# Expert rows combined at the end: the last two tiles by products on TensorE, the other row loads after the third-last tile

## The chip, the core and the metric

The kernel runs on one NeuronCore of a Trainium2 chip. Its engines are PE (TensorE, matrix products), DVE (VectorE), ACT (ScalarE), POOL (GpSimd) and SP (SyncE, which here only issues DMAs); 16 DMA engines move data between HBM and SBUF. The metric is the time of the whole program on the device in microseconds (us), as a median of several executions. "Span" is the time from the first to the last instruction of the one execution that was profiled.

## What is computed

A one-layer encoder block on 512 tokens of width 1024 in float32: RMS norm, a projection, a convolution branch and a sparse attention branch, gates, an output product, and then a mixture of experts, with a last RMS norm. What matters here is the end:

```
h = rms_norm(x, g_ffn)
x = x + hier_moe(h, ...)        # each token: 1 of 4 groups, 2 of its 8 experts
return rms_norm(x, g_final)

# hier_moe, for each token t and its two experts e with weights c[t, e]:
#   y[t] += c[t, e] * (silu(h[t] @ w_gate[e]) * (h[t] @ w_up[e])) @ w_down[e]
```

Each of the 32 experts has w_gate and w_up of 1024 x 256 and w_down of 256 x 1024.

## The kernel before, in words

Tokens stand in four blocks of 128 (TB = 4, one token per partition); `xr` ("x_rows") is the residual in SBUF, `wts[:, c, b]` the weight of choice c (0 or 1) of the tokens of block b. DVE computes the routing: for each token and choice the slot in a *tile*. A tile has 32 slots for each expert of a pair, so one tile serves one pair of experts; a pair has at least one tile, and there are 16 pairs. In this run 30 tiles are used. `tab[n]` is the number of tiles up to pair n in the order of work, read into registers by the engines ("TENSOR_LOAD tab"); `order` is the order of the pairs. The weights of a pair (4 MB for gate and up in eight loads of 512 KB, 2 MB for down in two of 1 MB) go into one of three slots; SP issues the loads of pair n when PE has finished with the pair n-3 (L400 and L410).

For each tile t, in a loop on every engine:
- POOL gathers the tokens' rows by an indirect DMA into `ring` ("bm", L582), some tiles ahead. Its tiny additions on `carrier` (L567) carry signals.
- DVE copies them to `xg` ("v_rows", L1608 for the first tile, L1613 in the loop). PE transposes them (L909), ACT and DVE evacuate half each (L1218, L1602, "kT").
- PE multiplies by gate and up (L932), ACT takes SiLU (L1225), DVE multiplies and so on (L1616, L1619), PE transposes once more (L941) and multiplies by down (L949) into `bank[2]`, of which each quarter of 32 partitions holds one expert's 32 slots by one half of 512 columns.
- ACT evacuates `bank[2]` to `ys` ("qT", L1229). POOL scatters it by an indirect DMA to `y_dram` ("expert_rows", L622), which has a row for each choice and token (row c * 512 + token). Indices beyond the bound write nothing; that is how empty slots are left out.

After the last tile (`tiles` in all):
- SP loads the final gain (L451, earlier, once the last pair but one has its tiles done), waits until the scatters of *all* tiles have landed (L454), loads the eight blocks of expert rows into `yrow` ("region", L457), and stores each block of the result when it is ready (L463).
- DVE adds `wts * yrow` to `xr` for each block and choice (L1627, 128 x 1024), and scales the finished block by `rs` and the gain (L1637): the left half, and the whole for the last block.
- ACT squares and sums a block (L1232) and scales right halves of blocks 0 to 2 (L1237), POOL computes the power -0.5 (L628) and multiplies those right halves by the gain (L633).
- PE has nothing to do.

The engines run their own programs in order and wait on semaphores. The order is that of the code; there is no scheduler.

## Time and profile before

| | |
|---|---|
| median of 3 executions | 682.74 us (681.72 to 686.35) |
| the profiled execution | 684.94 us, span 683.0 us |
| PE busy | 561.7 us, 82% of the span |
| DVE, ACT, POOL busy | 337.5, 256.9, 299.3 us |
| DMA moved | 149.21 MB |
| expert tiles, by PE's first and last instruction of them | 405.9 to 649.0 us |

Busy time is the time in which an engine executes instructions. A row of a timeline gives the start of an instruction (or of several alike), its duration, the engine, the line of the kernel and what it writes and reads. In brackets stands the idle time of the engine before it and what released it. SPq is SP's issuing of DMAs; its duration says nothing on when the data lands.

### The profile page before, as it was taken

The numbers are of one execution on the slowest core, as the hardware profiler recorded it, in microseconds if no ns is written. First come the engines' busy times: TensorE is split into PE (matmuls) and PEld (weight loads), VectorE is DVE, ScalarE is ACT, GpSimd is POOL, SyncE is SP. The second block draws the span as 40 slices with busy tenths as digits, with TensorE's granted clock in tenths as the row PEclk, the third lists the DMA queues.
The fourth block names the chain that finished last, engine by engine and source line by source line (L and its number), as shares of the span: only waits on it lengthen the run. The fifth ranks groups of instructions, "written<-read, shape, count | busy, mean of one in ns | idle before, by whom it ended". The sixth has DMA issues, their size and how long they took to land.

```text
span 683.0 us, 12246 instructions
## 1 busy us (share of the span) xinstructions
PE 561.7 (82%) x4275; PEld 380.6 (56%) x4276; DVE 337.5 (49%) x827; ACT 256.9 (38%) x440; POOL 299.3 (44%) x470
## 2 busy tenths in 40 slices
PE   3899999999999999999998218889889859697700
PEld 3577788876665777777888114444444424344300
DVE  4418999999988993477131641121211111021136
ACT  6335433245565746533224002334324314132212
POOL 5334334479995213355700043444534514333314
PEclk9999999999999998999996559999999989899955
DMA  9122723232202033034068978999899999999463
GB/s 293 40 92 63 240 68 108 78 89 74 74 13 62 1 123 124 9 116 154 4 243 322 412 279 319 408 407 410 310 409 410 408 408 409 401 408 390 189 249 124
DMA packets 58813, 149.21 MB, mean 218 GB/s; under 512 B 8660, under 2 KB 25044, under 8 KB 58782
## 3 DMA queue, kind: packets, MB, share of 16 engines
q1 hardware_dynamic: 53438, 139.89, 54.8%
q0 software_dynamic: 5200, 8.41, 3.4%
q10 hardware_dynamic: 144, 0.52, 0.3%
q8 instruction: 16, 0.26, 0.2%
q14 instruction: 15, 0.12, 0.0%
HBM read 145.37 MB, written 12.08 MB: 231 GB/s over the span
## 4 chain that ended last, share of the span: by engine, by line
PE 51%; DVE 19%; SPq 14%; DMA 6%; issue 5%; ACT 3%; POOL 2%; DVEq 0%; ACTq 0%; POOLq 0%
PE bank L667 26%; SPq L400 10%; PE bank L932 9%; PE bank L949 5%; DVE bm L1317 4%; DVE m L1316 4%; SPq L410 3%; DMA region<-in_w_e_down 3%; DVE conv_buf L1308 3%; PE bank L745 2%; PE bank L909 2%; PE bank L880 2%; PE bank L778 1%; PE bank L766 1%; DMA region<-expert_rows 1%
## 5 line engine op out<-in xcount | busy, mean ns | idle before, releaser
L667 PE MATMUL bank<-h_hi,w_part 128*128 128x512 f32 (+1 forms) x528 | 174.8, 400 | 3.2 <-DVE h_lo L1266 1.7
L517 POOL TENSOR_TENSOR w_part<-region,w_part 128x1024 fp32r<-128x1024 f32 (+1 forms) x52 | 109.7, 2111 | 149.2 <-ACT w_part L983 149.2
L667 PEld LDWEIGHTS bank<-h_hi,w_part 128*128 128x128 f32 (+1 forms) x528 | 98.3, 186 | 31.1 <-issue 8.2
L932 PE MATMUL bank<-region,kT 128*32 128x256 f32 x1536 | 94.0, 399 | 18.1 <-DMA region<-in_w_e_up 13.6
L667 PE MATMUL bank<-h_lo,w_part 128*128 128x512 f32 (+1 forms) x264 | 103.6, 392 | 0.0
L1616 DVE TENSOR_TENSOR mask_b<-mask_b,bank 128x128 f32<-128x128 f32 x30 | 8.6, 288 | 187.0 <-ACT mask_b L1225 99.4
L932 PEld LDWEIGHTS bank<-region,kT 128*32 128x32 f32 x1536 | 56.2, 115 | 63.1 <-issue 40.9
L983 ACT ACTIVATE w_part<-region 128x1024 fp32r<-128x1024 f32 (+1 forms) x52 | 48.0, 925 | 109.6 <-PE bank L667 109.4
L567 POOL TENSOR_TENSOR carrier<-mhalf 128x1 f32<-128x1 f32 x184 | 33.0, 196 | 122.8 <-ACT qT L1229 115.8
L1351 DVE SCALAR_TENSOR_TENSOR bank<-glu,cv,bank 128x256 f32<-128x256 f32 x196 | 78.6, 479 | 0.0
L949 PE MATMUL bank<-region,mask_b 128*32 128x512 f32 x384 | 46.2, 598 | 11.7 <-DVE mask_b L1619 10.8
L667 PEld LDWEIGHTS bank<-h_lo,w_part 128*128 128x128 f32 (+1 forms) x264 | 49.3, 187 | 9.9 <-issue 0.7
L1229 ACT ACTIVATE qT<-bank 128x512 f32 x30 | 17.9, 597 | 85.7 <-PE bank L949 85.7
L582 POOL DMA_INDIRECT bm<-h_rows,gi x35 | 37.2, 1064 | 5.3 <-issue 0.5
L1225 ACT ACT_TABLE_LOAD x30 | 38.5, 1283 | 0.5
L1225 ACT ACTIVATE mask_b<-bank 128x128 f32<-128x128 f32 x30 | 8.3, 277 | 77.9 <-PE bank L932 77.9
L622 POOL DMA_INDIRECT expert_rows<-qT,si x30 | 31.0, 1033 | 14.6 <-issue 14.6
L909 PE MATMUL bank<-ident,v_rows 128*128 128x128 f32 x124 | 23.5, 313 | 7.6 <-DVE v_rows L1608 7.6
L909 PEld LDWEIGHTS bank<-ident,v_rows 128*128 128x128 f32 x124 | 17.4, 209 | 20.1 <-issue 20.1
L949 PEld LDWEIGHTS bank<-region,mask_b 128*32 128x32 f32 x384 | 10.4, 109 | 30.2 <-issue 29.2
L525 POOL TENSOR_SCALAR bm<-glu,cv 128x512 f32<-128x512 f32 x17 | 26.6, 1565 | 0.9
L667 PE MATMUL bank<-o_part,w_part 128*128 128x512 f32 x96 | 25.9, 430 | 0.7 <-POOL w_part L517 0.7
(253 smaller groups left out, 864.2 us busy)
## 6 DMA issues: line engine op xcount, KB each, us to landing
region<-in_w_e_down SPq DMA_DIRECT2D x22, 1024.0 KB
region<-in_w_e_gate SPq DMA_DIRECT2D x44, 512.0 KB
region<-in_w_e_up SPq DMA_DIRECT2D x44, 512.0 KB
region<-in_w_in SPq DMA_DIRECT2D x16, 1024.0 KB, 6.0
gates<-in_w_e_gate SPq DMA_DIRECT2D x20, 512.0 KB
gates<-in_w_e_up SPq DMA_DIRECT2D x20, 512.0 KB
conv_buf<-in_w_e_down SPq DMA_DIRECT2D x10, 1024.0 KB
region<-in_w_out SPq DMA_DIRECT2D x2, 2048.0 KB, 7.8
```

The source lines that it names most:

```text
L400: sp.dma_start(w_gu[slot][:, e, m, half, :, :], w[0, bass.ds(pair * 2 + e, 1), rows, :].rearrange("a (p k) f -> p (a k) f", k=KD // 2))\
L517: g.tensor_tensor(unit_part(u, 1), unit_raw(u), unit_part(u, 0).bitcast(F32), ALU.subtract)\
L567: ins = g.tensor_tensor(carrier[:, n:n + 1], mhalf[:], mhalf[:], ALU.add)
L582: g.indirect_dma_start(out=ring[:, u, :], out_offset=None, in_=h2_halves, in_offset=bass.IndirectOffsetOnAxis(ap=gi1[:, u:u + 1], axis=0), ...
L622: g.indirect_dma_start(out=y_halves, out_offset=bass.IndirectOffsetOnAxis(ap=si1[:, q:q + 1], axis=0), in_=ys[:, q, :], in_offset=None, bo ...
L667: last = mm(out_, a_parts[p], b_parts[q], start=start and x_ == 0, stop=stop and x_ == 2)
L909: last = tr(bank[6 + k // 2][:, k % 2 * P:(k % 2 + 1) * P], view[:, k, :], ident[:])
L932: last = mm(bank[0][32 * c:32 * c + 32, 0:FF], xTs[:, k, at_:at_ + 32], w_gu[slot][:, e, :, half, k, j * P:(j + 1) * P], start=(half == 0 ...
L949: last = mm(bank[2][32 * c:32 * c + 32, :], hidT[:, at_:at_ + 32], w_dn[slot][:, e, j, n * BANK:(n + 1) * BANK], start=(j == 0), stop=(j = ...
L983: a(unit_part(u, 0), unit_raw(u), ACT.Copy).then_inc(S["w_hi"], 1)
L1225: a(sil, bank[0][:, 0:P], ACT.Silu).then_inc(S["silu_g"], 1)
L1351: ins = v.scalar_tensor_tensor(out_, shifted, cv[:, c, j:j + 1], so_far, ALU.mult, ALU.add)
```

## The change

What it does, part by part:
- **Routing, DVE.** `tab` gets one more entry, `early` = tiles - 2. Ahead of the first tile DVE takes the scatter indices of the last two tiles to `late_si` and makes their entries in `sidx` invalid, so that these two tiles' scatters write nothing. It clears a tile `no_rows` and builds `col_w`: for each block of tokens a 128 x 128 matrix with a token's weight at the column of its slot in the last two tiles.
- **POOL** writes zeros by two indirect DMAs to the rows of `y_dram` that belong to the last two tiles (semaphore `zeroed`), ahead of its loop. After the tiles it keeps the power alone.
- **PE** transposes `col_w` ahead of the first tile (ACT evacuates it to `place`). After the last tile it forms, for the blocks 0 to 2, `diag` (weights of choice 1 on a diagonal) times the rows of choice 1, and adds `place` times the rows of the last two tiles (`late`); for block 3 the latter alone. Each block is two products of 512 columns into two banks.
- **ACT** builds three `diag` ahead of the first product, evacuates the last two tiles to `late` in four pieces of 32 partitions, and keeps the squares at the end.
- **SP** waits for the scatters of all tiles but the last two, and for `zeroed`, and loads the rows; each load has a semaphore of its own. The last block is stored in two halves.
- **DVE** at the end adds the rows of choice 0 of all blocks and of choice 1 of block 3, adds the banks in halves of 512 columns, and does all of the scaling.

```diff
@@ sync
-            tiles = sp.value_load(tab[0:1, PAIRS:PAIRS + 1], min_val=PAIRS, max_val=MAXT - 1)
+            early = sp.value_load(tab[0:1, PAIRS + 1:PAIRS + 2], min_val=PAIRS - 2, max_val=MAXT - 3)
...
-                sp.wait_ge(scattered[n], ((tiles + (RING - 1 - n)) // RING) * 16)
+                sp.wait_ge(scattered[n], ((early + (RING - 1 - n)) // RING) * 16)
+            sp.wait_ge(zeroed, 32)
...
-            for b in range(TB):
+            for b in range(TB - 1):
                 sp.wait_ge(S["o_ready"], b + 1)
-                if b < TB - 1:
-                    sp.wait_ge(S["o_half"], b + 1)
                 sp.dma_start(out[0, b * P:(b + 1) * P, :], xr[:, b, :]).then_inc(st_out, 16)
+            for n in range(RING):
+                sp.wait_ge(scattered[n], ((early + 2 + (RING - 1 - n)) // RING) * 16)
+            for n in range(2):
+                sp.wait_ge(S["o_ready"], TB + n)
+                sp.dma_start(out[0, (TB - 1) * P:T, n * BANK:(n + 1) * BANK],
+                             xr[:, TB - 1, n * BANK:(n + 1) * BANK]).then_inc(st_out, 16)
@@ gpsimd
             gather(RING, 0)
+            pool.wait_ge(S["late_ready"], 1)
+            hold(5)
+            for u in range(2):
+                g.indirect_dma_start(out=y_halves,
+                                     out_offset=bass.IndirectOffsetOnAxis(ap=late_si[:, u:u + 1], axis=0),
+                                     in_=no_rows, in_offset=None,
+                                     bounds_check=last_row, oob_is_err=False).then_inc(zeroed, 16)
...
-                if b:
-                    pool.wait_ge(ld_gbc, 32)
-                    pool.wait_ge(S["o_scaled"], b)
-                    g.tensor_tensor(xr[:, b - 1, BANK:D], xr[:, b - 1, BANK:D], g_final_bc[:, BANK:D], ALU.mult)\
-                        .then_inc(S["o_half"], 1)
@@ tensor
+            pe.wait_ge(S["col_ready"], 1)
+            for b in range(TB):
+                last = tr(bank[5][:, b * P:(b + 1) * P], col_w[:, b, :], ident[:])
+            last.then_inc(S["place_mm"], 1)
             pe.wait_ge(S["x2_ev"], 2 * TB)
             transpose_tile(0)
...
+            def weighted_row(b):
+                pe.wait_ge(ld_y[b][1], 16)
+                if b == 2:
+                    pe.wait_ge(S["xtev_a"], early + 3)
+                    pe.wait_ge(S["xtev_v"], early + 3)
+                for n in range(2):
+                    mm(bank[late_banks[2 * b + n]][:], diag[:, b, :], y_row(b, 1)[:, n * BANK:(n + 1) * BANK],
+                       start=True, stop=False)
+            def late_rows(b):
+                for n in range(2):
+                    if late_banks[2 * b + n] == 2:
+                        pe.wait_ge(S["yev_a"], early + 3)
+                    mm(bank[late_banks[2 * b + n]][:], place[:, b * P:(b + 1) * P], late[:, n, :],
+                       start=(b == TB - 1), stop=True).then_inc(S["late_mm"], 1)
+            weighted_row(0)
+            weighted_row(1)
+            pe.wait_ge(S["yev_a"], early + 3)
+            late_rows(0)
+            late_rows(1)
+            weighted_row(2)
+            late_rows(2)
+            late_rows(3)
@@ scalar
+            act.wait_ge(S["place_mm"], 1)
+            a(place, bank[5][:], ACT.Copy).then_inc(S["place_ev"], 1)
             rows_T(0)
+            for b in range(TB - 1):
+                last = a(diag[:, b, :], ident[:], ACT.Copy, scale=wts[:, 1, b:b + 1])
...
+            for u in range(2):
+                hidden_gate(early + u)
+                for n in range(2):
+                    for e in range(2):
+                        at_ = 64 * u + 32 * e
+                        last = a(late[at_:at_ + 32, n, :], bank[2][32 * (2 * e + n):32 * (2 * e + n) + 32, :], ACT.Copy)
+                last.then_inc(S["yev_a"], 1)
@@ vector
+            v.tensor_copy(late_si[:], sidx[:, bass.ds(early, 2)])
...
+            v.memset(no_rows, 0.0).then_inc(S["late_ready"], 1)
+            link(v.tensor_tensor(col_hit, spread(col_code, 1, 2 * TB), spread(hic[:], 2, P), ALU.is_equal))
+            link(v.tensor_tensor(col_hit, col_hit, spread(wts[:, :, :].rearrange("p c b -> p (c b)"), 2, P), ALU.mult))
+            v.tensor_tensor(col_w, col_hit[:, 0:TB, :], col_hit[:, TB:2 * TB, :], ALU.add)\
+                .then_inc(S["col_ready"], 1)
...
+            for b in range(3):
+                add_row(b, 0)
+            for k in range(2):
+                add_late(k)
+            add_row(3, 0)
+            for k in range(2, 4):
+                add_late(k)
+            add_row(3, 1)
+            mean_square(2, 0)
+            dve.wait_ge(ld_gbc, 32)
+            scale_out(0, whole)
+            for k in range(4, 6):
+                add_late(k)
+            mean_square(2, 1)
+            scale_out(1, whole)
...
```

Three places of the built programs, engine by engine in program order. The first is DVE ahead of the first tile. Before the change, behind the weights (`wts`) stand a table load and the copy of the first gathered rows (bm to v_rows):

```order
L1597 TENSOR_TENSOR wts<-wts,glu 128x4
L1606 TENSOR_LOAD tab
L1606 ISA x2
L1608 COPY v_rows<-bm 128x512
L1602 COPY kT<-bank 128x256
```

In the changed kernel, behind its own table load and the copy to `late_si`, the same copy (now L1693) is preceded by these; qT holds `col_code`, `col_hit` and `col_w`, glu `no_rows`:

```order
L1673 TENSOR_SCALAR qT<-iota 128x32 x4
L1675 TENSOR_SCALAR hic<-hi,tend 128x8
L1676 SCALAR_TENSOR_TENSOR hic<-hic,posc 128x8
L1677 TENSOR_SCALAR dst<-iota,tend 128x48
L1678 SCALAR_TENSOR_TENSOR sidx<-dst,sidx 128x48
L1679 MEMSET glu 128x512
L1680 TENSOR_TENSOR qT<-qT,hic 128x1024
L1681 TENSOR_TENSOR qT<-qT,wts 128x1024
L1682 TENSOR_TENSOR qT<-qT 128x512
L1693 COPY v_rows<-bm 128x512
```

The copy of the first rows has moved behind nine further kinds of instructions. The second place is PE behind the last tile. It ended there before; in the changed kernel (region is `yrow` or `late`, glu is `diag` or `place`):

```order
L975 MATMUL bank<-region,mask_b 32x512 x8
L947 REGISTER_ALU
L947 COMPARE_AND_BRANCH
L986 TENSOR_LOAD tab
L986 ISA x2
L997 MATMUL bank<-region,glu 128x512 x4
L1010 REGISTER_ALU
L1005 MATMUL bank<-region,glu 128x512 x4
L997 MATMUL bank<-region,glu 128x512 x2
L1005 MATMUL bank<-region,glu 128x512 x4
```

Fourteen products of 128x512 are added. The third place is DVE at the end. Before the change (region is `yrow` or the gain, ss the mean of squares):

```order
L1627 SCALAR_TENSOR_TENSOR x_rows<-region,wts,x_rows 128x1024 x3
L1255 TENSOR_SCALAR ss<-ss 128x1
L1627 SCALAR_TENSOR_TENSOR x_rows<-region,wts,x_rows 128x1024
L1637 SCALAR_TENSOR_TENSOR x_rows<-x_rows,rs,region 128x512
L1627 SCALAR_TENSOR_TENSOR x_rows<-region,wts,x_rows 128x1024
L1255 TENSOR_SCALAR ss<-ss 128x1
```

and in the changed kernel:

```order
L1714 SCALAR_TENSOR_TENSOR x_rows<-region,wts,x_rows 128x1024 x3
L1722 TENSOR_TENSOR x_rows<-x_rows,bank 128x512 x2
L1714 SCALAR_TENSOR_TENSOR x_rows<-region,wts,x_rows 128x1024
L1722 TENSOR_TENSOR x_rows<-x_rows,bank 128x512 x2
L1714 SCALAR_TENSOR_TENSOR x_rows<-region,wts,x_rows 128x1024
L1324 TENSOR_SCALAR ss<-ss 128x1
L1728 SCALAR_TENSOR_TENSOR x_rows<-x_rows,rs,region 128x1024
L1722 TENSOR_TENSOR x_rows<-x_rows,bank 128x512 x2
L1324 TENSOR_SCALAR ss<-ss 128x1
L1728 SCALAR_TENSOR_TENSOR x_rows<-x_rows,rs,region 128x1024
```

Five whole-row adds stand where eight were, all of them ahead of the first scaling; the adds from the banks have come between, and the scaling takes whole rows.

## Rows read from the trace of the kernel before

**Rows 1.** The page: mean busy share of the DMA engines, tenths, 40 slices of 17.1 us.

```profile
DMA  9122723232202033034068978999899999999463
```

**Rows 2.** The chain that ended last, 560 to 684 us: start, us, what.

```profile
578.80 0.27 SPq L440
...
628.27 18.65 DMA region<-in_w_e_down
```

**Rows 3.** Stretches of one microsecond: busy time (count) by engine, PEclk, DMA share, GB/s.

```profile
640.00:641.00 1.00, 0.00 (x0) 0.00 (x0) 0.00 (x0) 0.98 (x2) 0.19 (x1) 1.00 0.45 176
...
646.00:647.00 1.00, 0.20 (x1) 0.00 (x1) 0.52 (x2) 0.02 (x1) 0.00 (x0) 1.00 0.06 25
...
665.00:666.00 1.00, 0.00 (x0) 0.00 (x0) 0.82 (x2) 1.00 (x3) 0.05 (x1) 0.50 0.62 250
666.00:667.00 1.00, 0.00 (x0) 0.00 (x0) 1.00 (x1) 0.41 (x1) 0.00 (x0) 0.50 0.03 12
```

**Rows 4.** Timeline of the end, all engines: start, us, engine, line, operation [idle before].

```profile
634.13 1.03 POOL L622 DMA_INDIRECT expert_rows<-qT,si  x1 [0.49 <-issue]
...
647.05 1.92 PE L949 MATMUL bank<-region,mask_b 128*32 128x512 f32 x16 [0.86 <-DMA region<-in_w_e_down]
...
649.17 0.60 ACT L1229 ACTIVATE qT<-bank 128x512 f32 x1 [3.15 <-PE bank L949]
...
653.52 3.87 SPq L457 DMA_DIRECT2D region<-expert_rows  x8
...
658.42 2.60 DVE L1627 SCALAR_TENSOR_TENSOR x_rows<-region,wts,x_rows 128x1024 f32<-128x1024 f32 x2 [11.90 <-DMA region<-expert_rows]
...
663.51 1.54 POOL L628 TENSOR_TENSOR rs<-ss,mhalf 128x1 f32<-128x1 f32 x1 [11.89 <-DVE ss L1255]
...
676.19 2.27 DVE L1637 SCALAR_TENSOR_TENSOR x_rows<-x_rows,rs,region 128x1024 f32<-128x1024 f32 x1 [0.66 <-POOL rs L628]
```

**Rows 5.** Timelines of the first expert tile: DVE, then PE, then POOL.

```profile
400.68 0.20 DVE L1597 TENSOR_TENSOR wts<-wts,glu 128x4 f32<-128x4 f32 x1
405.35 0.43 DVE L1608 COPY v_rows<-bm 128x512 f32<-128x512 f32 x1 [4.47 <-POOL carrier L567]
...
405.92 1.10 PE L909 MATMUL bank<-ident,v_rows 128*128 128x128 f32 x4 [7.55 <-DVE v_rows L1608]
408.37 5.56 PE L932 MATMUL bank<-region,kT 128*32 128x256 f32 x64 [1.34 <-DVE kT L1602]
...
418.32 0.19 POOL L567 TENSOR_TENSOR carrier<-mhalf 128x1 f32<-128x1 f32 x1 [4.50 <-ACT qT L1229]
```

**Rows 6.** Groups by shape: names, shapes, count | busy us, mean ns | idle before.

```profile
L807 PE MATMUL bank<-conv_buf,ones 128*128 128x512 f32 x8 | 3.7, 602 | 1.3 <-issue 1.3
...
L1480 DVE TENSOR_TENSOR x_rows<-x_rows,bank 128x512 f32<-128x512 f32 x8 | 5.2, 685 | 24.2 <-PE bank L667 24.2
L1491 DVE SCALAR_TENSOR_TENSOR gates<-x_rows,rs,qT 128x1024 f32<-128x1024 f32 x4 | 5.1, 1284 | 2.6 <-POOL rs L557 2.6
...
L991 ACT ACTIVATE ki_part<-bank 32x512 fp32r<-32x512 f32 x4 | 2.3, 584 | 0.0
...
L557 POOL TENSOR_TENSOR rs<-ss,mhalf 128x1 f32<-128x1 f32 x4 | 2.2, 543 | 19.2 <-DVE ss L1255 19.2
```

**Rows 7.** Time to landing of the expert scatters (L622), then of the stores (L463).

```profile
DMA to landing us min/median/max: 2.7/6.2/6.9
...
DMA to landing us min/median/max: 2.7/2.7/2.9
```

**Rows 8.** PE's granted clock (PEclk) in stretches around waits, columns as in rows 3.

```profile
408.00:412.00 4.00, 3.63 (x36) 2.04 (x40) 0.46 (x1) 0.32 (x1) 2.82 (x9) 0.50 0.26 72
412.00:416.00 4.00, 3.49 (x47) 1.84 (x41) 1.34 (x4) 0.66 (x2) 1.49 (x4) 0.97 0.68 246
...
620.00:624.00 4.00, 1.93 (x16) 0.43 (x16) 0.44 (x2) 1.72 (x2) 0.51 (x2) 1.00 1.03 397
...
651.00:653.00 2.00, 0.00 (x0) 0.00 (x0) 0.00 (x0) 0.00 (x0) 0.62 (x1) 0.55 0.10 33
```

More of the change, by code:

```diff
@@ new lines, in scale_out @@
+            def scale_out(b, cols):
+                dve.wait_ge(S["rstd_ready"], 2 * TB + b + 1)
+                v.scalar_tensor_tensor(xr[:, b, cols], xr[:, b, cols], rs[:, 2, b:b + 1], g_final_bc[:, cols],
+                                       ALU.mult, ALU.mult).then_inc(S["o_ready"], 1)
+            whole, halves = slice(0, D), (slice(0, BANK), slice(BANK, D))
+            next_rows(early + 1)
+            hidden(early + 1)
+            for b in range(3):
+                add_row(b, 0)
@@ new lines, in _ @@
+            for k in range(2):
[11 more added lines that the diff above has]
+            scale_out(1, whole)
+            for k in range(6, 8):
+                add_late(k)
+            mean_square(2, 2)
@@ L1641 @@
+            scale_out(2, whole)
+            mean_square(2, 3)
+            for cols in halves:
+                scale_out(3, cols)
 _INS = ["x", "g_mix", "w_in", "conv_w", "conv_b", "conv_ln_g", "conv_ln_b", "w_conv_out", "w_attn_out", "w_out",
```

86 lines of the change are left out of this document (53 added, 33 removed).

## The prediction, made before the changed kernel was run

> **What bounds the kernel now.** I read the page first, then the chain of waits, the table by stretches, and the timelines of the end and of the start of the expert tiles. Three things are to be seen.
>
> First, the weight stream. The page's DMA slices of 17.1 us stay at 8 or 9 tenths from about 410 us to 632 us, and it thins out some microseconds later [rows 1]. The first expert tile opens that stream (slots are free only after it), so whatever delays tile 0 delays the whole stream and its end by as much. In the chain the last two weight loads, issued at 628.27, take 18.65 us to land [rows 2].
>
> Second, those loads do not land together. At the end the DMA share falls slowly: 0.45 at 640 and still 0.06 at 646, the last with 25 GB/s [rows 3]. One engine of 16 is a share of 0.0625, and 0.06 at 25 GB/s is one engine at its full rate: some of the 16 are several microseconds behind the first ones. When the queue starts empty there is no such tail: the eight row loads of the end break off within one microsecond (0.62, then 0.03) [rows 3]. So the lag was collected over the long stream.
>
> Third, the end. The last tile's down product runs from 647.05 for 1.92 us, ACT evacuates at 649.17, the scatter follows, and only at 653.52 does SP begin the eight loads of expert rows; DVE gets its first pair at 658.42 and scales the last block from 676.19 for 2.27 us, to 678.46 [rows 4]. From there the last store and the closing take the rest of the 683.0 us, 4.54 us. So 29.4 us lie between the end of the last product (648.97) and the end of DVE. About 9.5 of them go to the evacuation, the scatter and the first row loads; the rest is a DVE chain of eight row adds of 1.28 us, with waits for POOL's power.
>
> **The head of the change.** DVE ends its weights work at 400.88, then idles 4.47 us until the first rows are there, and copies them at 405.35; PE transposes from 405.92, and the first products start at 408.37 [rows 5]. The change puts ahead of that copy: a table load (SP's of the same kind takes 0.27 us [rows 2] and what follows it some 0.15; 0.4); a copy of two columns and four of 32 columns, unchained (0.1 apart, 0.5; an estimate from the 0.20 us of a small op [rows 5]); four small ones of which three are chained (0.2 each, 0.75); a memset of 512 columns (no row; between 0.2, a small op, and 0.69, a 512-column add [rows 6]; I take 0.45); two passes over 1024 columns (1.28 each as the 1024-column row of L1491 [rows 6], 2.6 with the chaining); and a 512-column add, 0.69. Sum 5.4 us, so DVE is free at 406.3 and the copy starts 0.95 us later than now. PE then has four more transposes first: four take 1.10 us with the last one's 0.34 of latency, so 0.25 apart at this stage's clock. They start at about 406.45, the row transposes at 407.45 where they were at 405.92: 1.5 us later. ACT's evacuation of the places (0.6) ends at about 408.2, when it is needed for the rows. The three diagonals follow behind the rows and lie in ACT's wait for the first products, which run 5.56 us [rows 5]. **Head: +1.5 us**, in bounds of +0.9 (only the copy slips) and +3.
>
> POOL's two zeroing scatters cost 1.03 us each, as the scatter at 634.13 [rows 4], and stand ahead of its loop. It waits 4.50 us for ACT before its first real scatter [rows 5], so they hide; without that cover they would cost 2.3. Two late tiles' scatters now write nothing, and nobody waits for them but the last store.
>
> **The row loads.** SP now waits for the third-last tile's scatter, issued at 634.13 [rows 4] and landing some 6.2 us later [rows 7]: the loads are issued from 640.3, 13.2 us earlier than now. What is behind them on SP are only the stores. But they go through the same queue behind the weights, and a load counts only when all engines have delivered. The most backward engine is free at about 647.6 (last down weights and the final gain), and 512 KB take 1.3 us (eight in 10.4 us, 4.19 MB, 655 to 665.5, ending sharply [rows 3]). So the eight rows land on that engine's time: (0,0) 649.5, (0,1) 650.8, (1,0) 652.1, (1,1) 653.4, (2,0) 654.7, (2,1) 656.0, (3,0) 657.3, (3,1) 658.6. The Trainium skill (DMA: Bandwidth & Descriptors, "Latency and other measured facts") says that two of the 16 engines are usually slower, with traffic that GpSimd issues as its guess at the cause. By that rule the lag stays and the sum below holds; the trace shows laggards, not which they are.
>
> **The end, replayed** (times of the kernel before, without the head's 1.5).
> - ACT evacuates the last tile in four pieces of 32 partitions. The 32-partition row of L991 costs 0.584 [rows 6], no less than 128 partitions (0.60 [rows 4]): 649.17 to 651.5.
> - PE does 14 products of 128x128 by 128x512 in f32. The trace shows such a product as two instructions: four of them as the eight of L807, 3.7 us from the first start to the last end with 0.60 for the last [rows 6]; 3.1 / 7 is 0.44 an instruction and 0.87 a product, at full clock. The weighted rows of block 0 wait for row (0,1), 651.0 to 652.7; block 1 for (1,1), 653.6 to 655.3; then ten products without a pause, to 664.0. The first finished half of block 0 is there at 656.3, the last half at 664.0.
> - DVE adds rows (0,0), (1,0), (2,0) as they land, to 656.0; halves of block 0 (0.69 each, the add from a bank of L1480 [rows 6]) to 658.1; row (3,0), block 1's halves and row (3,1) to 662.2. Then per block: mean (0.15), POOL's power with its signals (0.75; the power alone 0.54 in the row of L557 [rows 6]), scaling of 1024 columns (1.28, L1491; now 2.27 beside POOL's halves, which are gone), and two half adds of the next. Block 0 is scaled at 664.5, block 1 at 668.15, block 2 at 671.75, and the two halves of block 3 at 673.4 and 674.15.
> - DVE thus ends 4.3 us earlier than 678.46. The last store is half as large: 0.4 less of its 2.7 us [rows 7], an estimate from 1.3 us per 512 KB.
>
> **Sum:** -4.3 -0.4 +1.5 = -3.2 us, against the profiled span of 683.0 (its execution took 684.94, the median of the three is 682.74). The predicted median is 682.74 - 3.2, 679.5.
>
> The reason why so little comes of loads that start 13 us earlier: they are still held by the last weights, and DVE, which lost three row adds (3 x 1.28) and POOL's and ACT's help, gained eight half adds (8 x 0.69) and the whole scaling. From the first half on it is the bound, 17.9 us.
>
> **The rivals.**
> 1. *The rows are not held back* by the lagging engines (their packets lie mostly on free ones, or those catch up). For it: the share of 0.45 at 640 means nine are free. Against: the sharp end at 665 shows an even spread. Then PE goes from 649.2 straight on, the first half is there at 653.5, 2.8 us earlier, and all after it: 676.7. Chance 0.2.
> 2. *Slower: PE's clock falls in the pause.* PE stands still from 648.97 to 651.0. Now the granted clock is full at 646 [rows 3], and 0.55 on average from 651 to 653 [rows 8], behind the last product. But from 620 to 624, where PE is busy for only 1.93 of 4 us, it stays at 1.00 [rows 8], which speaks against it. At 1.2 GHz all 14 products would take 1.74 us each, the last half would be there at 675.5 and DVE would end at 680.8: 6.6 us more, 686.1. It decides (slower than before) once about 10 of the 14 run at the lower level; at the start of the tiles the clock came back within 4 us of the first products (0.50 to 412, then 0.97) [rows 8], which covers two or three. Chance 0.08.
> 3. *The head costs more.* POOL's power took 1.54 us at 663.51 beside DVE's row add where it takes 0.54 alone [rows 4, 6]: DVE's long passes can hold up POOL's small ones before the first gathers. If POOL's signal that releases the first copy falls behind two such passes, or DVE's passes behind POOL, it is 1 to 2.5 us more: 680.5 to 682. The Trainium skill (SBUF — State Buffer, "Who interferes with whom") has it that a VectorE instruction with two SBUF inputs and a GpSimd one that reads SBUF exclude each other; the two new passes are such. It agrees with the 1.54, and speaks against the change at just this place. Chance 0.15.
> 4. *The change does not do what it says:* the early loads slow the last weights, or the third-last scatter lands much later. The queue is first come, and free engines do not take the lagging one's rate; 0.05, at 682 to 684.
>
> **How the numbers follow.** The forecast as summed, 678 to 681.5, has 0.52. Range 675.5 to 684.0: it takes in rival 1 with a head of only 0.9, rivals 3 and 4, the memset's and the copy's bounds, and leaves rival 2's worst out. A measurement of this kernel can tell about 1% from no change. Faster by over 1% (under 675.9) needs rival 1 with a cheap head or an earlier clock rise at tile 0: 0.13. Slower by over 1% (over 689.6) needs more than rival 2 whole: 0.03. Within 1%: 0.84.
>
> **What would show it.** In the changed profile: the copy of the first rows 0.9 to 1.0 us and the first products about 1.5 us later; the last tile's down product later by the same; the row loads issued near 640 plus 1.5; the first DVE row add *not* before the last tile's products have ended; four evacuations of 0.58; 28 product instructions 0.44 apart and clock 1.00; DVE without a gap over 1 us from the first half add to the end. If the rows are all there before 649, rival 1 is right; if they stand 0.87 apart, rival 2. The prediction is wrong in size if DVE's instructions at the end sum to more than 17.9 us.

## The result, and the profile after

The changed kernel took 674.53 us in the median of four executions (669.89 to 679.34), the kernel before beside it 683.38: a ratio of 0.988, interval 0.984 to 0.993. The forecast of 679.5 missed: the median lies 1 us under the low end of its range, 675.5. The four executions are two at 679 and two at 670. The profiled one is of the upper pair, 679.34 us with a span of 677.5 against 683.0 before. So two things have to be found: where 5.5 us of span went in the profiled pair, and what the other 9 us are that some executions have and others do not.

**The head** of the changed kernel, ahead of the first tile (timeline: start, us, engine, line, operation, [idle before <- what ended it]):

```profile
399.40 0.20 DVE L1667 TENSOR_TENSOR wts<-wts,glu 128x4 f32<-128x4 f32 x1
...
400.66 0.17 DVE L1670 COPY late_si<-sidx 128x2 uint32 x1 [1.06 <-issue]
...
402.56 1.16 DVE L1680 TENSOR_TENSOR qT<-qT,hic 128x1024 f32<-128x1024 f32 x1
403.76 1.23 DVE L1681 TENSOR_TENSOR qT<-qT,wts 128x1024 f32<-128x1024 f32 x1
404.50 0.53 POOL L588 TENSOR_TENSOR carrier<-mhalf 128x1 f32<-128x1 f32 x1 [2.08 <-DMA bm<-h_rows,gi]
...
405.63 0.42 DVE L1693 COPY v_rows<-bm 128x512 f32<-128x512 f32 x1
...
405.77 1.11 PE L937 MATMUL bank<-ident,qT 128*128 128x128 f32 x4 [8.67 <-DVE qT L1682]
...
406.67 1.06 PE L931 MATMUL bank<-ident,v_rows 128*128 128x128 f32 x4
...
408.64 1.94 PE L958 MATMUL bank<-region,kT 128*32 128x256 f32 x16 [0.90 <-DVE kT L1688]
```

All of this execution is 1.28 us early here (the weights end at 399.60, before at 400.88 [rows 5]), from a stretch that the change does not touch. Counted from there, the copy of the first rows is 1.56 us later than before, and the first products, 408.64 against 408.37 [rows 5], are 1.55 later.

**The end**, same view:

```profile
642.63 3.78 SPq L474 DMA_DIRECT2D region<-expert_rows  x8
...
649.96 2.39 ACT L1302 ACTIVATE region<-bank 32x512 f32<-32x512 f32 x4 [2.56 <-PE bank L975]
650.31 1.28 DVE L1714 SCALAR_TENSOR_TENSOR x_rows<-region,wts,x_rows 128x1024 f32<-128x1024 f32 x1 [2.40 <-DMA region<-expert_rows]
...
651.73 1.96 PE L997 MATMUL bank<-region,glu 128*128 128x512 f32 x4 [1.84 <-DMA region<-expert_rows]
...
653.05 1.35 DVE L1714 SCALAR_TENSOR_TENSOR x_rows<-region,wts,x_rows 128x1024 f32<-128x1024 f32 x1 [1.45 <-DMA region<-expert_rows]
...
655.55 1.28 DVE L1714 SCALAR_TENSOR_TENSOR x_rows<-region,wts,x_rows 128x1024 f32<-128x1024 f32 x1 [1.15 <-DMA region<-expert_rows]
...
657.20 1.48 DVE L1722 TENSOR_TENSOR x_rows<-x_rows,bank 128x512 f32<-128x512 f32 x2 [0.37 <-PE bank L1005]
...
661.22 3.60 PE L1005 MATMUL bank<-region,glu 128*128 128x512 f32 x8
...
663.35 1.28 DVE L1728 SCALAR_TENSOR_TENSOR x_rows<-x_rows,rs,region 128x1024 f32<-128x1024 f32 x1 [0.77 <-POOL rs L656]
...
664.56 1.28 DVE L1722 TENSOR_TENSOR x_rows<-x_rows,bank 128x512 f32<-128x512 f32 x2
...
666.56 1.28 DVE L1728 SCALAR_TENSOR_TENSOR x_rows<-x_rows,rs,region 128x1024 f32<-128x1024 f32 x1 [0.66 <-POOL rs L656]
...
671.76 1.42 DVE L1728 SCALAR_TENSOR_TENSOR x_rows<-x_rows,rs,region 128x512 f32<-128x512 f32 x2 [0.66 <-POOL rs L656]
```

The last down product starts at 647.97 in this trace, 0.92 us later than the 647.05 of [rows 4]. Add 0.92 to the replay of the prediction and it meets the rows of this trace to a tenth: rows (0,0), (1,0), (2,0) were put at 649.5, 652.1, 654.7, so 650.4, 653.0, 655.6 (measured 650.3, 653.05, 655.55); the first half at 656.3, so 657.2 (657.20). The loads were issued 1.4 us later than the replay has them (642.63, where 640.3 and 0.92 make 641.2), and it made no difference: they wait 7.7 us for the first pair. The stretches (PE busy, PEclk, DMA share, GB/s) show what holds them: the queue is full to 654, and then single engines are still at work:

```profile
650.00:651.00 1.00, 0.00 (x0) 1.00 1.05 418
653.00:654.00 1.00, 0.69 (x2) 1.00 1.03 410
655.00:656.00 1.00, 1.00 (x3) 1.00 0.20 82
658.00:659.00 1.00, 1.00 (x3) 1.00 0.04 16
```

Behind the first half the replay is too slow: DVE ends at 673.18, 15.98 us behind the first half add, not 17.9.

### The profile page after: what moved, and what is told of

It reads as the page before. It is cut to its first block, busy times and chain, and to the rows that moved or that the text cites. A ratio compares the mean times of both kernels' runs of the same rounds, so it can differ in the third digit from the quotient of the medians.

```text
span 677.5 us, 12329 instructions
## 1 busy us (share of the span) xinstructions
PE 573.9 (85%) x4305; PEld 385.9 (57%) x4308; DVE 342.7 (51%) x847; ACT 257.6 (38%) x445; POOL 296.1 (44%) x470
## 4 chain that ended last, share of the span: by engine, by line
PE 53%; DVE 21%; SPq 11%; DMA 6%; issue 4%; ACT 3%; POOL 1%; DVEq 0%; POOLq 0%; ACTq 0%
PE bank L689 26%; PE bank L958 10%; SPq L416 8%; PE bank L975 5%; DVE bm L1386 4%; DVE m L1385 4%; DVE conv_buf L1377 3%; DMA gates<-in_w_e_up 3%; PE bank L767 2%; SPq L426 2%; PE bank L902 2%; PE bank L931 2%; DMA region<-expert_rows 2%; PE bank L800 1%; PE bank L788 1%
## 5 line engine op out<-in xcount | busy, mean ns | idle before, releaser
L958 PE MATMUL bank<-gates,kT 128*32 128x256 f32 x384 | 23.3, 396 | 5.3 <-DMA gates<-in_w_e_up 4.4
L1385 DVE MAX8 m<-bm 128x8 f32<-128x256 f32 (+2 forms) x45 | 25.3, 562 | 1.6
```

What stands on the lines that cost most here:

```text
L958: last = mm(bank[0][32 * c:32 * c + 32, 0:FF], xTs[:, k, at_:at_ + 32], w_gu[slot][:, e, :, half, k, j * P:(j + 1) * P], start=(half == 0 ...
L1385: link(v.max(m8[:], src[:, 0:n]))
```

## The two groups of executions

The router stage lies ahead of anything the change touches. PE transposes a block of tokens and forms its 36 logits, four blocks in turn. The profiled execution of the changed kernel (PE's timeline):

```profile
357.95 1.04 PE L674 MATMUL bank<-ident,gates 128*128 128x128 f32 x8
360.79 1.13 PE L674 MATMUL bank<-ident,gates 128*128 128x128 f32 x8 [1.80 <-ACT conv_buf L1263]
361.76 2.33 PE L902 MATMUL bank<-wr,conv_buf 128*128 128x36 f32 x16
363.90 1.95 PE L674 MATMUL bank<-ident,gates 128*128 128x128 f32 x8
365.64 3.47 PE L902 MATMUL bank<-wr,conv_buf 128*128 128x36 f32 x16
```

and its stretches:

```profile
356.00:360.00 4.00, 2.99 (x18) 1.00 0.19 43
360.00:364.00 4.00, 3.21 (x25) 0.88 1.06 339
364.00:368.00 4.00, 4.00 (x21) 0.50 0.95 328
```

PE pauses 1.80 us for ACT, and the granted clock falls during the small products to 0.50, the 1.2 GHz level; then 16 of them take 3.47 us. In the trace of before it falls as well, and PEclk is 0.56 from 364 to 368. (A stage that keeps the full clock is called *held* from here on.) If this were what parts the groups, work for PE in the pause should move executions from one to the other.

**Experiment 1: the changed kernel again.** No edit.

> The changed kernel, unchanged, to see how its time is spread. Its four first executions fell in two groups, 679 us (span 677.0 to 677.5, mean granted clock 0.942) and 670 us (span 668.1, clock 0.957). Theory A: the groups differ in the router's stage, before anything the change touches: in the trace of 677.5 us the clock falls to its lower level at 363 us and PE's router products take 6.9 us for 32 where 16 take 2.3 us at the full level; an execution that keeps the full clock there is some 9 us shorter. It expects the groups again, and in a trace of the fast group the first expert tile 8 to 10 us earlier, with the tail as long in both. Theory B: the groups differ in the changed tail (rows that land early or late, the clock in the last products). It expects the first tile at the same time and the tail 9 us shorter.

Measured: 678.87 us in the median of 12 (672.2 to 682.9), ratio 0.992 (0.989 to 0.995). Three of 12 lie at 672 to 674, nine at 678 to 683. So the 674.53 of four executions caught two from the rarer group. The trace, of 680.13 us, has the router at half clock, so that it compares nothing between the groups. But it shows something at the end that the first trace does not. PE's pause behind the last down product is 2.03 us there (1.84 before), and the clock falls behind it and is back only at 656 (timeline, then stretches as above):

```profile
651.61 5.43 PE L997 MATMUL bank<-region,glu 128*128 128x512 f32 x8 [2.03 <-DMA region<-expert_rows]
...
652.00:653.00 1.00, 1.00 (x3) 0.83 1.02 406
654.00:655.00 1.00, 1.00 (x2) 0.50 0.49 185
```

The first half add stands 10.35 us behind the start of the last down product, where it was 9.23, and the end is 1.1 us later.

**Experiments 2 and 3: keep PE at work in the pause**, in the kernel before and in the changed one. Eight products of 512 columns into an unused bank:

```diff
@@ def transpose_rows
                         last.then_inc(mm_sem, 1)
+                    if after and b == 0:
+                        for k in range(8):
+                            mm(bank[5][:], m_hi[:, k, 0:P], m_hi[:, k, :], start=True, stop=True)
```

> The kernel before with eight products of 512 columns added in PE's 1.8 us pause ahead of the second block of the router's transposes; their result is not used. Theory A: if the clock stays at its upper level through the router's stage, the time falls by 8 to 10 us to about 674, in every execution. If the stage's own products are too thin to hold the clock, it falls a few microseconds later than now and the gain is 1 to 4 us. Theory B: no change (682 to 684).

> The changed kernel with the same eight products. Theory A: all executions in the fast group, 669 to 671 us, and then the difference to the kernel before with the same eight products is that of the change alone, 4 to 5.5 us. Theory B: the two groups of 679 and 670 us remain.

Measured: before_keep 680.14 us (0.995, 0.993 to 0.998), after_keep 671.98 (0.984, 0.979 to 0.990). Both traces have the router at full clock; this is after_keep's:

```profile
357.06 2.09 PE L679 MATMUL bank<-m_hi 128*128 128x512 f32 x8
359.11 1.14 PE L674 MATMUL bank<-ident,gates 128*128 128x128 f32 x8
360.08 1.87 PE L905 MATMUL bank<-wr,conv_buf 128*128 128x36 f32 x16
361.79 1.10 PE L674 MATMUL bank<-ident,gates 128*128 128x128 f32 x8
```

From the stage's start to the rank products behind it (L914 of the changed kernel; they count tokens for the routing) it is 19.6 us instead of 26.1, and the changed kernel's executions lie together at 670 to 675. That PE's clock in this stage sets a level of its own is shown. Before_keep gained 2.8 us where 8 to 10 were expected, so the two kernels with the products are 8.2 us apart, not 4 to 5.5; seven of its ten spans lie at 677.0 to 679.2. I took that for a clock that did not hold each time, hence the next runs.

**Experiments 4 to 8: a stronger hold**, three more such products behind each of the next two blocks' transposes (`if after and b < 3: for k in range((8, 3, 3)[b])`), in before, in the changed kernel, and in a version with a reordered end (that of experiment 14).

> The kernel before with fourteen products of 512 columns in the router stage that no result uses: eight in PE's pause ahead of the second block's transposes, three more behind the second block's and three behind the third block's (about 0.65 us each three). Theory that the two groups of executions differ by PE's granted clock in the router stage alone: with the stronger hold nearly all executions have the stage at full clock and lie 5 to 7 us under the kernel before's usual 682 to 683, at 675 to 678, and the scatter shrinks to one group. Rival, that the clock falls for a reason that PE's work there does not touch: 681 to 685 with a few at 676, as it was with eight products.

> The changed kernel with the same fourteen products. Theory: all executions in one group at 671 to 674; against the kernel before with the same products this gives what the change is worth with the router stage alike in both: 3 to 5 us less (forecast 3.2, the measured pieces say 4 to 5). Rival, that the change itself is worth more (8 us, as the difference of the two kernels' fast and slow groups would have it): 667 to 669 against 676.

> The changed kernel with the reordered end (gain's load behind the row loads, PE's late products of a block between its early ones, DVE's sums of the first halves ahead of the third block's) and the same fourteen products. Theory: the two gains add, 1 to 2 us under the changed kernel with the fourteen products, so 670 to 672 and the fastest of all kernels here. Rival, that the reordered end's gain of 1.5 us in one trace was chance: the same as the changed kernel with the products, within 0.5 us.

Measured: before_hold 680.61 us, after_hold 672.52, better_hold 673.10, beside 681.25. All three traces hold the clock. Three expectations fell. Better_hold was to be 1 to 2 us under after_hold and is not; its rival came true. Before_hold was not at 675 to 678: its trace has a span of 678.4 with the clock held, so before_keep's times did not show what I read from them. And the difference of the pair, 8.1 us, was that of the rival. So I took both again.

> The kernel before with the fourteen products again, for a second trace. Theory that the start of the router stage (356.0 to 359.4 us in the traces so far) depends on the execution alone, through clock dips at 18 to 24 and 268 to 276 us: this trace may have it anywhere there, and from PE's rank products to the first tile's first product it takes 25.0 +- 0.2, from there to the last down product 238.4 to 239.9, and from that to the end 35.2 to 36.0. Rival, that the kernel before is later there by its own code: 359 again.

> The changed kernel with the fourteen products again. Theory: rank products to first product 25.1 to 25.3 (the work on weights at the head is hidden behind the gather of the first rows when the router stage was fast), last down product to the end 29.0 to 29.6; against the kernel before with the products 5.5 to 6.5 us faster in the median. Rival, that the changed kernel is faster ahead of the router stage too: router stage at 356 again and 8 us in the median.

Measured: before_hold 677.8 (0.995, 0.992 to 0.998), after_hold 673.41 (0.986, 0.982 to 0.990) beside 681.57: a difference of 4.4, less than the 5.5 to 6.5 expected. Over both, the median of 21 is 679.5 and that of nine 672.8, 6.7 us apart. The trace of before began the router stage at 359.1 again, as the rival there had it, and that of the changed kernel at 357.9, not at 356.

**Experiments 9 and 10: both kernels unchanged**, for one more trace of each on one chip.

> The kernel before as it is. A second trace: the router stage at half clock as in the first (rank products 26 us behind the stage's start, first product 23.0 behind them), or held (20 and 25). By the theory that the groups are those of the router stage, executions lie near 682 or near 676, and the trace's group goes with its time.

> The changed kernel as it is, for its third trace, on the chip of before_again. Theory: near 678.5 (router stage at half clock, first product 24.5 behind the rank products) or near 671 (held, 25.2); in the median 4 us under the kernel before within the slower group. If the trace falls into the faster group it shows PE's clock at 1.00 to 368 us.

Measured: before_again 681.73 us, after_third 678.03 (0.994, 0.991 to 0.997). The traces fell into neither level I had named, at spans of 676.9 and 673.8, with the router at half clock. They began the router stage at 354.6 us, where the earlier traces have 356.0 to 359.4. So a third thing differs from execution to execution, the start of that stage. This table is worked out from the PE rows of each trace: start of the router stage (first transposes), from there to the rank products, to the first tile's first product, from there to the last tile's down product, and from that to the end of the span.

```
kernel          span   router  ->rank  ->first ->last down  ->end
before          683.0  359.34  26.06   22.97   238.68       35.95
before_again    676.9  354.57  26.87   22.28   237.96       35.22
before_keep     676.0  356.28  19.33   25.26   239.89       35.24
before_hold     678.4  359.02  20.73   25.00   238.41       35.24
before_hold_b   678.1  359.12  20.72   25.00   238.09       35.17
after           677.5  357.95  26.11   24.58   239.33       29.53
after_again     678.3  357.92  26.53   24.40   238.80       30.65
after_third     673.8  354.65  26.83   24.52   238.93       28.87
after_keep      669.9  356.26  19.58   25.16   239.92       28.98
after_hold      670.2  356.04  20.72   25.17   238.98       29.29
after_hold_b    671.6  357.88  20.72   25.11   238.96       28.93
```

1. The stage's start (354.6 to 359.3) follows PE's clock from 18 to 24 us and from 265 to 280, where the change has nothing: 1.00 and 1.00 in both traces that start at 354.6, 1.00 and 0.77 in those at 357.9, 0.72 and 0.77 at 359.34.
2. The router's own length has two levels, 26 to 27 us and 19 to 21. This is the larger part of the two groups.
3. The tail takes 35.2 to 36.0 us in the kernels before and 28.9 to 30.7 in the changed ones; the middle values differ by 6.1.
4. The head costs 1.6 and 2.2 us with the router at half clock, and with it held next to nothing (25.1 to 25.2 against 25.0 to 25.3).

The best matched pair is before_again and after_third, whose router stages start and run alike: +2.24 at the head, +0.97 through the tiles, -6.35 at the end, and 676.9 to 673.8, which is -3.1. The forecast was -3.2. Two held traces match as well, before_keep and after_keep (356.28 and 356.26): -0.10 at the head, +0.03 through the tiles, -6.26 at the end, and 676.0 to 669.9, which is -6.1.

The +0.97 is not all chance. In the first tile the 64 products by gate and up take 5.56 and 5.06 us in the two traces of the kernel before, and 6.38, 6.04 and 5.67 in those of the unedited changed kernel: PE's clock comes back later (PEclk is 0.50 until 414 in the first trace of the changed kernel, until 412 in that of before). With the router held both kernels have 5.0 to 6.2. So with the router at half clock the head seems to cost some 0.6 us more than its delay; why the clock is later is not shown.

Point 4 has its cause in the DMA. From the end of the weights (`wts`) to the copy of the first rows DVE's new work takes 6.0 us, 399.60 to 405.63, and the same in the other traces with the router at half clock. It costs what it exceeds the idle time that the kernel before has there: 4.47 us in its first trace, 3.81 in before_again, where the weights thin out sooner. That is the 1.6 and the 2.2. In before_hold the routing is ready 5.7 us earlier than in before, but the first rows are not (POOL's signal, start 401.68; before 405.13, so 3.5):

```profile
395.02 1.30 POOL L582 DMA_INDIRECT bm<-h_rows,gi  x1 [0.19 <-issue]
...
401.68 0.18 POOL L567 TENSOR_TENSOR carrier<-mhalf 128x1 f32<-128x1 f32 x1 [3.67 <-DMA bm<-h_rows,gi]
401.89 0.43 DVE L1611 COPY v_rows<-bm 128x512 f32<-128x512 f32 x1 [6.68 <-POOL carrier L567]
```

The gather stands with the prefetched expert weights, which keep the engines full until about 402 in both traces (before_hold):

```profile
398.00:400.00 2.00, 0.00 (x0) 0.50 1.03 411
400.00:402.00 2.00, 0.00 (x0) 0.50 1.03 399
402.00:404.00 2.00, 1.10 (x4) 0.50 0.87 342
```

DVE's idle time ahead of the copy is then 6.68 us instead of 4.47, and the change's new work goes into it. In after_hold 0.64 of it is left, so it is just covered:

```profile
399.05 0.43 DVE L1696 COPY v_rows<-bm 128x512 f32<-128x512 f32 x1 [0.64 <-POOL carrier L588]
```

## The parts of the change, one at a time

**Experiment 11: the head alone.** The kernel before with DVE's new block (the invalid indices go to a spare tile, so all tiles are scattered), POOL's two zeroing scatters, PE's transposes, ACT's copy and diagonals; the end as before.

```diff
-            v.scalar_tensor_tensor(sidx[:], dst[:], ...
+            v.scalar_tensor_tensor(spare[:], dst[:], ...
```

> The kernel before with the change's work ahead of the tiles (table load, matrix of weights, its four transposes, the diagonals, two zeroing scatters) and the tail of before, which uses none of it. Theory: the first products start 1.5 us later against the last step of the routing, all later work shifts by as much, total +1.5 us (+0.9 to +2.4, since the clock may rise later in the first tile's products). Rival: the weight stream absorbs the delay, total within 0.5 us.

Measured: 684.23 us, ratio 1.006 (1.002 to 1.009) beside 681.44. The medians differ by 2.8 us, more than the 1.5 expected and above its range of 0.9 to 2.4, though the interval reaches down to 1.5. From the rank products to the first product its trace has 24.57 us, 1.60 more than before and 2.29 more than before_again. So nothing hides the head while the router is at half clock. The rest of the 2.8 us lies behind the first product: the tiles take 239.10 us (238.68 and 237.96) and the end 36.19 (35.95 and 35.22), of which this one trace shows no cause but 0.2 to 0.7 us in the first tile's products.

**Experiment 12: the row loads wait for all tiles again**, the rest of the changed kernel kept:

```diff
-                sp.wait_ge(scattered[n], ((early + (RING - 1 - n)) // RING) * 16)
+                sp.wait_ge(scattered[n], ((early + 2 + (RING - 1 - n)) // RING) * 16)
```

> The changed kernel, but SP waits for all tiles' scatters before it loads any rows; nothing else is changed. Theory: the early start of the loads is what carries the gain. The loads are issued near 655.5 instead of 642.6 (last scatter issued at 653.1, and it writes nothing), the first pair is there near 660, the first finished half near 666 instead of 657, DVE ends 9 to 10 us later: 688 us, slower than the kernel before, which has less on DVE. Rival: the gain is in the combining on PE and the loads are hidden: less than 3 us later (under 682).

Measured: 688.0, 688.0 and 690.0 us, ratio 1.013 (1.006 to 1.020).

```profile
655.04 4.63 SPq L474 DMA_DIRECT2D region<-expert_rows  x8
658.78 1.28 DVE L1714 SCALAR_TENSOR_TENSOR x_rows<-region,wts,x_rows 128x1024 f32<-128x1024 f32 x1 [11.41 <-DMA region<-expert_rows]
...
667.85 1.48 DVE L1722 TENSOR_TENSOR x_rows<-x_rows,bank 128x512 f32<-128x512 f32 x2 [1.72 <-PE bank L1005]
```

The loads start 12.4 us later, and the first row is there 3.7 us behind the issue instead of 7.7: with the weights gone the queue is fast. So 12.4 us of earlier issue bring 8.5 at the first row and 10.6 at the first half add (667.85 against 657.20). Most of the 2.1 us between the two is the clock's: PE has stood still for 10.8 us, its first eight products take 6.75 us, 0.85 apart, and PEclk is 0.50 until 666. So the edit changes two things, but even without these 2 us it would be slower than the kernel before (681.44). Without the earlier loads the new way of summing costs more than it saves.

**Experiment 13: second rows of the blocks 0 to 2 back on DVE**, the last two tiles on PE as changed:

```diff
@@ tensor
-            weighted_row(0)
-            weighted_row(1)
             pe.wait_ge(S["yev_a"], early + 3)
             late_rows(0)
             late_rows(1)
-            weighted_row(2)
@@ vector
             for b in range(3):
                 add_row(b, 0)
+                add_row(b, 1)
```

> The changed kernel with the second rows of blocks 0 to 2 added by DVE as before, not by diagonals on PE; the last two tiles' rows still on PE. DVE gets three row adds more (3 x 1.28 us), of which the waits of 1.45 and 1.15 us for rows that land late can hide two. Theory (arrival of the rows bounds the first part, DVE the rest): DVE's first half add is at 658 instead of 657.2 and the end is 0.5 to 1.5 us later. Rival (DVE is the bound all through): 3.8 us later. Third: PE was the bound, and the end is earlier.

Measured: 678.74 us (0.996, 0.993 to 1.000), eight of ten at 677.6 to 681.3 and two at 672. Its trace has the router held:

```profile
641.50 1.28 DVE L1713 SCALAR_TENSOR_TENSOR x_rows<-region,wts,x_rows 128x1024 f32<-128x1024 f32 x1 [2.30 <-DMA region<-expert_rows]
642.97 1.28 DVE L1713 SCALAR_TENSOR_TENSOR x_rows<-region,wts,x_rows 128x1024 f32<-128x1024 f32 x1 [0.18 <-DMA region<-expert_rows]
...
644.47 5.25 DVE L1713 SCALAR_TENSOR_TENSOR x_rows<-region,wts,x_rows 128x1024 f32<-128x1024 f32 x4 [0.22 <-DMA region<-expert_rows]
649.75 1.28 DVE L1721 TENSOR_TENSOR x_rows<-x_rows,bank 128x512 f32<-128x512 f32 x2
```

DVE adds the six rows with hardly a wait. From the last down product to the end it is 30.64 us, against 28.93 to 29.29 in the held traces of the changed kernel. So the diagonals are worth 1.4 to 1.7 us of the tail's 6 (0.5 to 1.5 was expected); the rest is the last two tiles' places and the earlier loads together, for the loads can only be early if the places are there. The trace has another use: its router code is that of the changed kernel, unedited. Its span of 669.9, less those 1.4 to 1.7 us, would be 668.2 to 668.5, and the two executions at 670 have spans of 668.1.

**Experiment 14: a reordered end.** The gain's load goes behind the row loads, so that it does not stand ahead of them on the DMA engines that lag; PE forms a block's late rows right behind its weighted row; DVE adds block 0's and block 1's halves ahead of the third block's row.

```diff
@@ tensor
             weighted_row(0)
-            weighted_row(1)
             pe.wait_ge(S["yev_a"], early + 3)
             late_rows(0)
+            weighted_row(1)
             late_rows(1)
@@ vector
-            for b in range(3):
-                add_row(b, 0)
-            for k in range(2):
-                add_late(k)
+            add_row(0, 0)
+            add_row(1, 0)
+            add_late(0)
+            add_late(1)
+            add_row(2, 0)
...
```

> The changed kernel with three moves in the tail: the gain's load behind the row loads instead of ahead of them; on PE each block's late rows directly behind its weighted rows; on DVE the half adds and row adds of the next block put between a block's mean and its scaling, so that POOL's power is hidden. Expected by the trace of the changed kernel (times of the slow group, last down product at 648): rows 1.3 us earlier, first half add at 654.5 instead of 657.2, DVE without a wait of more than 0.3 us but for the last block, end 3.5 to 4.5 us earlier: 675 us in the group of 679, and 666 where the router's stage keeps the full clock. If the rows keep their times, the lagging engines were not held up by the gain's load and 1 us less is won.

Measured: 677.51 us, ratio 0.995 (0.991 to 0.999). From the last down product to the end 28.05 us, and 28.10 in better_hold: about 1 less than the 28.9 to 29.5 of most of the changed kernel's traces, where 3.5 to 4.5 was expected. The first half add did come 3.6 us earlier (5.66 us behind the down product's start, where it was 9.23). Of this 1.3 us is a row add that now comes behind it, and 0.8 more is given back in waits (DVE's chain from there takes 18.06 us, where it was 15.98):

```profile
652.21 1.48 DVE L1722 TENSOR_TENSOR x_rows<-x_rows,bank 128x512 f32<-128x512 f32 x2 [0.69 <-PE bank L1005]
...
655.57 0.69 DVE L1722 TENSOR_TENSOR x_rows<-x_rows,bank 128x512 f32<-128x512 f32 x1 [0.45 <-PE bank L1005]
...
657.31 0.58 POOL L656 TENSOR_TENSOR rs<-ss,mhalf 128x1 f32<-128x1 f32 x1 [4.56 <-issue]
...
660.74 1.52 POOL L656 TENSOR_TENSOR rs<-ss,mhalf 128x1 f32<-128x1 f32 x1 [2.85 <-DVE ss L1324]
```

DVE now waits for PE and for POOL's power, one of which takes 1.52 us beside a DVE row add. The first row is added 0.99 us behind the down product's start (0.73 in better_hold), where the six traces of the changed kernel have 1.46 to 2.40; that fits the gain's load having stood ahead of the rows, but one edit with three moves does not show it. In the median better_hold (673.10, 670.5 to 673.4) does not differ from after_hold. Both are over 8 us under the kernel before beside them, a part of which is the held router's, and after_hold is the version I would keep: the change with fourteen products that hold the clock (0.987, 0.985 to 0.989, and 0.986 again).

## Why the prediction was right and wrong

- **The weight stream and the lagging engines: right.** The rows landed at the forecast instants to 0.1 us in the first trace, and with them the first half, 9.23 us behind the start of the last down product. That it fits so closely is in part luck: four other traces of the changed kernel have 8.6 to 8.9. Rival 1 (rows not held back), which had the first half 2.8 us earlier, is out in all of them.
- **The head: right in size in the first trace, by two errors that cancel.** +1.5 forecast, +1.55 in the first trace, +2.24 in the matched pair, 2.8 us in the medians of experiment 11, nothing with the router held. That its cost depends on how long the weights hold up the first gather was not in the prediction. The table load left DVE idle for 1.06 us, not 0.4, and the copy slipped 1.56 us instead of 0.95; from the row transposes to the products it was 1.97 us instead of 2.45. Of rival 3 a mild form is there: POOL's signal took 0.53 us beside DVE's passes where it took 0.18 (1.19 in after_again). The Trainium skill (SBUF — State Buffer, "Who interferes with whom") has the two exclude each other; the trace agrees with its direction. The third gather was issued 6.50 us behind the first where it was 5.29 before; the copy of the first rows did not wait, as DVE was busy with its own passes for 0.6 us longer.
- **The clock in PE's pause: right in five traces of the changed kernel, wrong in one.** In the first trace PEclk is 1.00 from 645 to 664, and 28 product instructions stand 0.43 to 0.44 apart (eight in 3.60). In after_again it fell behind a pause of 2.03 us, and rival 2 came in part: 1.1 us, not its 6.6, because the clock was back at 656, and what follows is bound by DVE and not by PE.
- **The DVE chain at the end: mis-sized, 17.9 forecast, 15.98 measured.** "Two half adds of the next" were priced 1.38 and the instruction behind them starts 1.19 us after their start (664.56, 665.75); the scaling of 1.28 is followed after 1.21, and mean and power, priced 0.90, take 0.81. A block's cycle is 3.2 us (663.35, 666.56, 669.76), where the prediction's own instants (664.5, 668.15, 671.75) stand 3.6 apart. With 0.8 saved ahead of the first scaling it is 1.9 us in all, saved against the sum. The last store gave back some: 4.32 us from DVE's end to the end of the span where it was 4.54, 0.2 less and not 0.4.
- **The span's account:** forecast -3.2; measured -5.5 = -1.28 ahead of everything, +1.55 head, +0.65 through the tiles, -6.42 from the last down product on, where the forecast had 0, +1.5, 0 and -4.7. So of the 2.3 us beyond the forecast 1.7 are the tail's, and the 1.28, which the change does not make, is half undone by the tiles. The first tile's products alone took 0.82 more; over all traces the stretch has 238.0 to 239.9 in either kernel.
- **The comparison of medians: the step that failed.** "The predicted median is 682.74 - 3.2" took one level for the kernel's time, and gave the clock ahead of the change no term. It has levels that lie ahead of the change: half or full clock in the router, and the early dips. In the larger samples of the unedited kernels the change is worth 4.1 us (678.87 against 682.93) and 3.5 us (678.03 against 681.57), near the forecast, and both those medians lie in its range. With the router held it is worth more, about 6 by the table and 4.4 to 8.2 by medians, because the head is then covered. The first four executions had two at 670, held ones by all that the other runs show, and that made 674.53; neither the mis-sized chain nor the head would have taken it out of the range.

**What stays open.** Why a program's executions hold the clock at all, and how often: of the changed kernel 5 of 25 executions lie under 674 us, of the kernel before none in about a hundred, though on one chip five of 25 lie at 675.6 to 678.2, with spans of 673.8 to 675.4. Before_again's trace has the earliest start of the router stage, at half clock, and a span of 676.9 still, so an early start alone would not make those five; held ones they may be, but none was traced. No trace caught the unchanged `after` itself with the router held; that its 670s are this is inferred from after_keep's trace and from second_rows_dve's, whose router code is the same and unedited. And whether the kernel's own code has a share in the early dips: three of five traces of the kernel before (with its products or without) start the stage at 359.0 to 359.4, none of the changed kernels' ten does. Of the 8.1 us of the first held pair its traces put 3.0 there.

## What to carry to other kernels

Before a difference of 1% is read off a pair of traces, cut both into stretches at events that both have, and compare each stretch: one of them may differ by more than the change is worth, where the change has nothing. A cost put ahead of a wait is free only while the wait's releaser is the later one; here the same 6 us of DVE work cost 2.2 us or next to nothing, depending on whether the routing or the weight stream was late. A median of four executions of a program with two levels says little; 12 put it 4.3 us higher. And loads that queue behind a long stream gain less than their earlier issue: 12.4 us earlier gave 8.5.

## What the runs showed of the hardware

- The clock fell during transposes and 36-column products behind a pause of 1.8 us, in all traces of unedited router code but one (second_rows_dve), and held in all seven with eight or fourteen 512-column products put in. PE counted as busy (4.00 of 4 us) at half clock as at full.
- At the end, the clock held through pauses of PE of 0.96 to 1.84 us in five traces of the changed kernel, and was at 0.50 within 2 us of new work behind one of 2.03 in after_again; behind 10.8 us, in experiment 12, it was at 0.50 from the start and came back after 6 us of products.
- Half adds from a bank, back to back, take 0.64 us each where one alone is 0.69; a 32-partition evacuation takes 0.60 (four in 2.39), as 128 partitions do.
- A value load on DVE left it idle for 1.06 us, in the changed kernel's traces and in experiment 11's alike.
- POOL's one-column power takes 0.54 us alone and 1.51 to 1.54 beside a DVE row add, in the kernel before and in experiment 14.
